# Forgetting attention: a step's filler matmuls between its scores and its values instead of behind its later turns

## What is computed

```python
def forgetting_attention(q, k, v, lf):
    cT = jnp.cumsum(lf, axis=1).transpose(0, 2, 1)
    ...
    def block(args):          # one block of 128 queries
        s = jnp.einsum('bqhd,bkhd->bhqk', qi, k) * scale
        s = s + (ci[..., :, None] - cT[..., None, :])
        s = jnp.where(qpos[:, None] >= kpos[None, :], s, -jnp.inf)
        p = jax.nn.softmax(s, axis=-1)
        return jnp.einsum('bhqk,bkhd->bqhd', p.astype(v.dtype), v)
```

## Time and profile before

| | |
|---|---|
| median of 3 runs | 2748.34 us (2747.95 to 2749.74) |
| the profiled execution | 2748.69 us, of it 2746.9 us between the first and the last instruction |
| TensorE busy | 2686.9 us, 98% |
| VectorE, ScalarE, GpSimd busy | 1084.0, 956.7 and 636.4 us |
| the stage of the change | about 1476 to 1680 us |
| mean granted clock of TensorE | 0.991 |

### The profile page before, as it was taken

How to read it: one execution, slowest core, us unless ns; L and a number is a source line. 1 busy time by engine, 2 the same in 40 slices (tenths; PEclk the granted TensorE clock), 3 DMA queues, 4 the chain that set the end, 5 groups by cost and what they waited for, 6 DMA issues and landing times.

```text
span 2746.9 us, 33279 instructions
## 1 busy us (share of the span) xinstructions
PE 2686.9 (98%) x13699; PEld 2267.3 (83%) x13699; DVE 1084.0 (39%) x1353; ACT 956.7 (35%) x1502; POOL 636.4 (23%) x278
## 2 busy tenths in 40 slices
PE   7899999999999999989999999999999999999999
PEld 6688898898888888878888898888888888788887
DVE  3466624644223232835534765434243122131223
ACT  4466631112222114536635665334332122021122
POOL 1111112221222223222211225222502222222221
PEclk9899999999999999999999999999999999999999
DMA  3000011111111114131112124210201111111112
GB/s 131 24 24 24 33 38 46 46 47 39 47 50 47 46 50 153 39 110 39 47 39 89 51 93 161 77 54 30 85 9 54 51 50 46 47 46 54 46 47 92
DMA packets 43714, 158.10 MB, mean 58 GB/s; under 512 B 5092, under 2 KB 5476, under 8 KB 42808
## 3 DMA queue, kind: packets, MB, share of 16 engines
q1 hardware_dynamic: 38624, 131.29, 14.2%
q10 hardware_dynamic: 4952, 24.82, 2.4%
HBM read 141.19 MB, written 10.70 MB: 55 GB/s over the span
## 4 chain that ended last, share of the span: by engine, by line
PE 89%; issue 3%; ACT 3%; DVE 3%; POOL 1%; DMA 1%; ACTq 0%; POOLq 0%; DVEq 0%
PE ps L727 38%; PE ps L812 17%; PE ps L833 5%; PE ps L1319 4%; PE ps L1581 3%; PE ps L1406 3%; PE ps L1002 2%; PE ps L932 2%; PE ps L1059 1%; PE ps L1348 1%; PE ps L1473 1%; PE ps L1443 1%; PE ps L1025 1%; PE ps L786 1%; PE ps L1335 1%
## 5 line engine op out<-in xcount | busy, mean ns | idle before, releaser
L576 POOL TENSOR_TENSOR w_lo<-w_raw,w_hi 128x1024 fp32r<-128x1024 f32 x206 | 502.7, 2441 | 1809.7 <-ACT w_hi L1720 1809.4
L727 PE MATMUL ps<-A_lo,w_hi 128*128 128x512 f32 (+1 forms) x1560 | 434.1, 366 | 2.4 <-issue 2.4
L727 PE MATMUL ps<-A_hi,w_hi 128*128 128x512 f32 (+1 forms) x1560 | 435.3, 367 | 0.0
L727 PE MATMUL ps<-A_hi,w_lo 128*128 128x512 f32 (+1 forms) x1560 | 433.4, 366 | 0.0
L1720 ACT ACTIVATE w_hi<-w_raw 128x1024 fp32r<-128x1024 f32 x206 | 217.3, 1055 | 492.6 <-PE ps L812 332.5
L727 PEld LDWEIGHTS ps<-A_lo,w_hi 128*128 128x128 f32 x1560 | 275.8, 189 | 50.2 <-issue 2.8
L727 PEld LDWEIGHTS ps<-A_hi,w_hi 128*128 128x128 f32 x1560 | 275.7, 189 | 48.8 <-issue 1.9
L727 PEld LDWEIGHTS ps<-A_hi,w_lo 128*128 128x128 f32 x1560 | 276.1, 189 | 47.5
L3203 DVE TENSOR_TENSOR X<-ps,X 128x512 f32<-128x512 f32 x96 | 66.4, 692 | 369.6 <-PE ps L812 291.7
L812 PE MATMUL ps<-w_hi,U_hi 128*128 128x512 f32 x448 | 174.3, 389 | 0.0
L812 PE MATMUL ps<-w_lo,U_hi 128*128 128x512 f32 x448 | 174.3, 389 | 0.0
(11 more groups left out here) (502 smaller groups left out, 5166.6 us busy)
## 6 DMA issues: line engine op xcount, KB each, us to landing
w_raw<-in_units SPq DMA_DIRECT2D x208, 512.0 KB, 3.2
X<-in_x ACTq DMA_DIRECT2D x4, 1024.0 KB, 12.6
X<-in_x ACTq DMA_DIRECT2D x1, 4096.0 KB, 15.0
x_spill<-X ACTq DMA_DIRECT2D x1, 4096.0 KB, 12.2
X<-x_spill ACTq DMA_DIRECT2D x1, 4096.0 KB, 14.3
out<-lnf_xn SPq DMA_DIRECT2D x8, 512.0 KB, 2.6
w_raw<-in_units SPq DMA_DIRECT2D x12, 256.0 KB, 2.6
mx_inv<-inverse_rows SPq DMA_DIRECT2D x8, 256.0 KB, 3.4
```

The source lines that it names most:

```text
L576: nc.gpsimd.tensor_tensor(w_lo[:, slot, :], w_raw[:, slot, :], w_hi[:, slot, :].bitcast(F32), ALU.subtract).then_inc(w_lo_ready, 1)
L727: last = nc.tensor.matmul(out, w[:, slot, o:o + m], v[:, k, cols] if k is not None else v[:, cols], start=(first and j == 0 and q == 0), s ...
```

## The change

One call is moved up by two statements, in the loop over heads and steps. For each step the filler piece k + 1 is issued on TensorE behind the scores of step k + 1, ahead of the values of step k - 1 and of the later turns. No other line changes.

```diff
                     elif h + 1 < HEADS:
                         fx_scores(h + 1, 0)
+                    fx_fill(4 * h + s + 1)
                     if s or h:
                         fx_values(*((h, s - 1) if s else (h - 1, 3)))
                     fx_turn(h, s, range(2, j + 1))
-                    fx_fill(4 * h + s + 1)
```

## The result

The changed kernel takes 2767.68 us (median of 3 runs, 2766.45 to 2768.01), the kernel before 2748.34: 1.0072 times as long, with a 95% interval of 1.0058 to 1.0086. The prediction was 2768.6, slower.

A forecast was written before the change was run, and what follows sets the result against it. TensorE, 98% busy, was taken to bound the kernel. Chunk 4's 9.5, chunk 9's 8.0, fillers' 2.25 and the row's last turn's 0.5, less 0.3 us, made 19.95 on 2748.69: 2768.6 us, range 2760 to 2778.

The forecast's parts named there:

- Nothing to win: In the changed stage TensorE waits only 2.0 us in all, so the new order cannot give back more.
- The cover in the kernel before: Chunk 4 started 3.65 us behind chunk 2, covering the 2.06 us way from transposes to low part with 1.6 to spare.
- Chunk 4: Directly behind chunks 2 and 3, it waits for chunk 2's low part: 1.19 us in each of 8 heads, 9.5 us.
- Chunk 9: Step 3's turn waits for chunk 7's low part: 0.99 us in each of 8 heads, 8.0 us.
- The fillers' own waits: Moved fillers wait for the keys' copy or low parts in steps 26, 28, 30 and 31: 2.25 us; step 1's nothing.
- The sum: All new waits in the stage less 0.3 us given back in head 0: 19.95 us, giving 2768.6 us.
- The clock: TensorE's granted clock stays at 1.00 through the stage, nothing charged; one possible fall in step 31 would cost 1.7 us.
- The signs named: Profile after: about 16 turn waits, 14 us; head period about 27.3 us; ScalarE not waiting for the filler; clock 1.00.
- (A): Clock falls in every second wait of chunks 4 and 9: 13.6 us more, 2782 us; chance 0.06.
- (B): Waits travel on to the next head's first turn, up to 0.8 us a head: 6 us more, 2775 us; chance 0.10.
- (C): A chunk's way is not the bound, turn waits vanish: 2747 to 2749 us, not slower; chance 0.02.
- (D): Later turns hide about half, 0.6 us a wait instead of 1.1: 12 us, 2761 us; chance 0.12.

The follow-up runs named there:

- an experiment: Changed kernel with VectorE's order altered in steps 0 and 2, low parts of the later turns ahead of the taking of the values: 2774.41 us.
- the doubled low part: VectorE writes the low part of chunks 2 and 7 twice: 2779.99 us on the changed kernel, 2748.23 us on the kernel before.
- the three partial moves: Kernel before with the filler moved only in step 0, only in step 2, or only in steps 1 and 3: 2758.41, 2753.66 and 2751.47 us.

## Why the prediction was right

- **Nothing to win.** Right: the stage had 2.0 us of waits, and the trace shows no other idle time of TensorE there.
- **The cover in the kernel before.** Right that it was enough, wrong in how much was to spare. The prediction took the way of 2.06 us from head 0 and set it against 3.65 us. In the kernel before the probabilities stand ahead of chunk 2's and chunk 7's high parts on ScalarE; chunk 7's low part was there only 0.5 us before chunk 9 started. The sum doesn't use this number, since behind the early filler the probabilities are done in time.
- **Chunk 4.** 1.19 us a head was predicted, from 2.06 - 0.87. Measured 2.11 - 0.87 = 1.24, 9.9 us in place of 9.5. The 2.06 had been read in head 0 from chunk 0 to chunk 2. The prediction's side calculation, VectorE free at 1.1 and the high part there at 1.2 us, is in the rows above: 1.09 and 1.24.
- **Chunk 9.** Predicted 0.99, measured 0.91 and 0.96: 7.5 us in place of 8.0. The way is 1.67 us in place of 1.70, and the small delay by the taking of the values, 0.05 us, is there only in every second head.
- **The fillers' own waits.** Step 28's 0.4 and the row's turn (0.6 us more idle, 0.5 predicted) are as predicted; steps 26 and 30 cost 0.2 each (0.3 and 0.1 predicted); step 31's filler starts 3.25 us behind chunk 77 (3.4 predicted). Step 1's filler shows no idle time in any head, with so little to spare that an experiment used it up.
- **The sum.** 19.95 us for the stage was predicted, 19.9 measured without the clock. So close an agreement is in part luck: chunk 4 was 0.4 us too low and chunk 9 0.5 too high.
- **The clock.** It was charged nothing, with one fall in step 31 as a possibility at 1.7 us. It did fall there, at 1.56 us. The 2768.6 holds to a microsecond because the stage's fall was made up behind the stage, where a fall of the kernel before did not come again. That is luck of the run and no part of the argument. What brings the fall in step 31 is open: it came in both traces of the changed kernel and was gone when step 31 was left as before, but it was also missing in a run with nearly the same two waits. The fall at 1937 us is no matter of the change as far as the traces show: the wait of 1.9 us ahead of it (L1637) is in the changed kernel too, and in the kernel before with the doubled low part, which has the old order on TensorE, the wait is there and the fall is missing as well.
- **The signs named.** 16 waits, 14.8 us (14 predicted); a head in 27.33 us (27.3); no first turn of a head waits for probabilities but that of head 0, as before; ScalarE waited 14.9 us for the filler in 14 times before and 3.1 in one time now. The one sign that did not hold is the clock of 1.00 through the whole stage; the fall begins at about 1690.7 us, just behind the 1476 to 1690 us in which a fall was to count against the forecast.
- **Rivals.** (A), a fall in every second wait, did not come at 0.7 to 1.1 us; falls came after some of the waits when they were 1.7 to 1.8 us long. The Trainium skill's remark on PSUM-queue cycling (TensorE: Matmul & The Clock Gate, "A second HAM failure mode: psum-queue depth-cycling") is so not borne out by the 16 short waits; the falls behind longer ones, and behind some pairs of short ones, are in line with it. (B), waits that travel, is excluded by the head's period of 27.33 us and by the turns' waits of the three partial moves, (C) by the doubled low part, (D) by the size of the 16 waits.

## What to carry to other kernels

Before moving a piece of work that "only fills", list the pairs of instructions between which it stands and write down the length of the way that each pair needs (here 2.1 and 1.7 us against 0.87 and 0.76 us of turns). On an engine that is never idle, a filler placed where nothing waits is worth nothing, and the same filler between two turns of one bank is worth the part of the way that nothing else covers. Half of it was enough for the turns here, but the piece that moves has waits of its own: moved in the odd steps only, it made the stage 5.4 us longer without one new wait of a turn for a low part. Read a late start from the starts and not from the idle time, which was 0.17 us less for chunk 4, and none at all where chunk 9 came 0.3 us late. And before another piece is put in its place, read the written order of the engines that serve the way, since a cover that stands ahead in their queue becomes part of the way.

## What the runs showed of the hardware

One wait of TensorE of 0.7 to 1.1 us with dense work about it left the granted clock at 1.00 in every head. Two close together, with 0.5 us of turns between, brought the level of 1.2 GHz for about 3.4 us where they were 0.80 and 0.98 us (two traces of two), and did not where they were 0.74 and 1.04 us (one trace). Of single waits of 1.79 us, two of seven were followed by a fall in one run (the doubled low part) and all three in another (the values behind the turns). A wait of 1.9 us behind the stage is the same in the traces of the kernel before and of the changed kernel, and only the first has the fall behind it. So the length of a wait alone does not decide it.

One such fall costs 1.6 us. The falls behind the stage (near 1937 and 2391 us in the kernel before) differ from trace to trace, and the faster runs of one kernel have the higher mean clock: with half the filler left behind, the runs at 0.994 took 2746.1 and 2747.4 us, those at 0.991 took 2752.0 to 2752.7. That the falls make up most of such a spread is likely by these numbers, but was not tried by itself.
